# Dummy products first, x split from its banks, an earlier lambda, and a last residual with tokens on partitions

## The chip, the cores and the metric

One core of one Trainium2 chip runs the whole program. The time is device microseconds of one execution; the kernel before takes 1857.08 us (median of 3 runs, 1857.0 to 1858.16).

## The reference

Three pre-norm transformer layers over x (512 tokens, width 1024), all in fp32. What the change touches, cut to that:

```python
# layer 1: forgetting attention beside a multiscale pool, then a gated FFN
h = rmsnorm(x, norm1_g); proj = h @ w_in            # q, k, v, forget logits, pool input u
x = x + concat(attn, pool) @ w_out
x = x + (silu(h2 @ w_gate) * (h2 @ w_up)) @ w_down;  x = rmsnorm(x, final_g)
# layer 2: differential attention; lam needs only four parameter vectors
lam = exp(sum(lq1*lk1)) - exp(sum(lq2*lk2)) + 0.2
a = softmax(s0) - lam * softmax(s1);  o = (a @ v);  x = x + norm(o) @ w_o
# each of layers 2 and 3 ends in a convolutional FFN
x = x + (silu(g) * val) @ w_down                     # w_down: 2816 x 1024
return rms_norm(x, final_norm_g)                     # last step of all
```

## The kernel before

x lies transposed in `XT` (features on partitions, 8 tiles of 128 x 512). Every fp32 product is made of three fp32r products (high x high, high x low, low x high), so each weight chunk and each activation tile is split in a high half (ACT, `whi`/`hi`, lines 1855 and 1859) and a low half (DVE, `wlo`/`lo`, lines 1685, 1676, 1691). Weights come in chunks of up to 128 x 1024 through 2 raw buffers `RAW` and 3 split buffers `WH`/`WL`; SP loads chunk n+2 once `wlo` of chunk n is done. `gemm_f` (lines 1552 to 1554) takes 4 feature blocks of 512 tokens per chunk; `gemm_t` (lines 1580 to 1582) puts tokens on partitions.

All work is written as generators that yield steps. A planner (`run`) gives every step an estimated begin and duration (`takes`, `LAG`) and emits, engine by engine, the one that can begin first, by rank among those that begin within 60 to 100 ns. The result is one fixed order for each engine: an engine executes its steps in that order and waits at the head of its queue if the plan was too hopeful. DMA issues sit in SP's queue in the same emission order.

- Start. PE waits for the identity first of all. `x_in(f)` turns four 128 x 128 blocks of x into a bank (`x_turn`), copies the bank to `XT` (`x_copy_v` or `x_copy_a`), and only then `Norm.feed` makes the halves from `XT` (`make`) and the squares. SP issues x quarter 0, chunk 0 (2 k-blocks), quarter 1, chunk 1, quarters 2 and 3, then some 20 small loads, then chunk 2. Squares are added up on POOL (`acc`, line 1980), `sums` (line 1614) reduces them on PE, `root_in`, `root_exp`, `root_out` make the reciprocal root.
- Pool stretch of layer 1 (about 155 to 185 us). After the last products of the norm, `ev_pool` runs `scaled` (DVE), sliding sums on POOL (`window`, line 1999), `less` and `lo` on DVE for each of four groups; the residual of the first attention group adds 8 banks into `XT` (`add`, line 1697); then `mix` (4 products) and the splits of its banks, on which the next residual waits.
- `lam_sums()` (line 1409 in `products`) is spawned as layer 2 begins: four broadcast loads (line 1533), `lam_in` (two reductions of 128 x 64, line 1813), `lam_exp` (ACT), `lam` (three small DVE operations, lines 1819 to 1822). DVE and ACT wait for its results in line.
- End. The last `ffn` calls `residual`: 144 products into 8 banks, 8 `add`s, 8 squares and POOL sums for the last norm, then `way_out`: `out_turn` (32 transposes of `XT`), 8 `out_scale`s on DVE and 8 stores of 256 KB.

Of the kernel before, what the change touches and what calls it, by code (L numbers as in the profile page):

```python
# [42 lines left out]
    "x_turn": {"pe": 1}, "x_copy_a": {"act": 1}, "x_copy_v": {"dve": 1},  # L43
# [15 lines left out]
    "out_turn": {"pe": 1}, "out_scale": {"dve": 1},  # L59
# [77 lines left out]
def takes(kind, eng, f):  # L137
# [9 lines left out]
    if eng == "pe":  # L147
        if kind == "gemm_f":
            return 3 * len(f["xs"]) * mm(512)
        if kind == "gemm_t":  # L150
            return 3 * len(f["xs"]) * mm(f["width"])
# [11 lines left out]
    if eng == "act":  # L163
# [6 lines left out]
        return {"whi": 1060.0, "tap2": 805.0, "silu": 625.0, "tok_qk": 890.0, "tok_q": 584.0, "tok_k": 482.0, "o_copy": 683.0,  # L170
                "key_row": 710.0, "root_exp": 450.0, "lat_sq": 660.0, "consts": 510.0, "vec": 220.0, "cvec": 470.0, "tok_f": 270.0,
                "gate_exp": 500.0, "lam_exp": 210.0}.get(kind, 600.0)
    if eng == "dve":
        if kind == "lo":
            n = width_of(f["src"])
            return dve(n) if f["scale"] is None else 1.45 * dve(n) if f["src"].shape[0] == P and n == S else 1.1 * dve(n)
# [4 lines left out]
        if kind == "p_two":  # L181
            return 420.0 + 440 + 1.55 * width_of(f["p1"])
        return {"wlo": 1273.0, "add": 682.0, "tap1": 743.0, "tap0": 743.0, "settle": 745.0, "diag": 880.0, "root_in": 165.0,
                "root_out": 760.0, "both_in": 370.0, "both_out": 370.0, "eighth": 170.0, "lam_in": 500.0, "lam": 500.0,
                "gate_in": 400.0, "gate_log": 190.0, "kv_mean": 170.0, "q_root": 170.0, "fg_cols": 160.0}.get(kind, 690.0)
# [5 lines left out]
def build(nc, a, out):  # L191
    with ExitStack() as ctx:
# [183 lines left out]
        def halves(dst_h, dst_l, src, after, scale=None, free=()):  # L376

            hi = yield step("hi", dst=dst_h, src=src, scale=1.0 if scale is None else scale, after=counts([*after, *free]))
            lo = yield step("lo", dst=dst_l, src=src, high=dst_h, scale=scale, after=[hi.act])
            return lo.dve  # L380

        def split_pair(pair, src, after, scale=None, rows=slice(0, P)):
            h, l = pair.h, pair.l
            lo = yield from halves(R[rows, h.i, :], R[rows, l.i, :], src, after, scale, h.free + l.free)
            pair.ready = [lo]
            return lo
# [17 lines left out]
        def plan_qk(w, g, qo, ko):  # L404
            for k in range(0, 8, 2):
                chunk(2, 512, (0, wap(w, k * P, 2, qo + g * 256, 256)), (256, wap(w, k * P, 2, ko + g * 256, 256)))
# [18 lines left out]
        def plan_ffn(part, pieces, down):  # L425
# [3 lines left out]
            plan_rows(down, PARTS[part][0] * 256, 2 * len(PARTS[part]))  # L429

        for g in (0, 1):
            plan_qk(w_in, g, 0, 512)
# [32 lines left out]
        for part in range(len(PARTS)):  # L465
            plan_ffn(part, ((up2[1], 0), (up2[1], 2816)), dn2[1])

        landed, lands, w_split, w_low, w_used = [], {}, {}, {}, {}
        raw_cnt = [0] * NRAW
# [11 lines left out]
        def high_weights(which):  # L481
            for n in which:
                while n >= NSP and n - NSP not in w_used or n >= NRAW and n not in lands:
                    yield None
                free = [w_used[n - NSP]] if n >= NSP else []
                w_split[n] = yield step("whi", n=n, after=[(s_raw[n % NRAW], landed[n]), *free])

        def low_weights(which):
            for n in which:
# [3 lines left out]
                lo = w_low[n] = yield step("wlo", n=n, after=[st.act])  # L493
# [53 lines left out]
        def root(x, n, inv_d, after):  # L547

            v, l, y, c, o = (small(n) for _ in range(5))
            st = yield step("root_in", x=x, v=v, inv_d=inv_d, after=counts(after))  # L550
            st = yield step("root_exp", v=v, l=l, y=y, after=[st.dve])
# [3 lines left out]
        class Norm:  # L555
# [11 lines left out]
            def feed(self, f):  # L567
                if self.split:
# [5 lines left out]
            def make(self, f):  # L574
                yield from fill(self.X[f])
                sc = self.cols[:, f:f + 1] if self.cols is not None else col(self.g + f)
                yield from split_pair(self.X[f], XT[:, f, :], x_done[f], sc)
# [116 lines left out]
        def landing(s, t):  # L694
# [6 lines left out]
                   for s in range(2) for hh in range(4) for x in range(2)]  # L701
# [4 lines left out]
        for q in range(4):  # L706
            landing(s_x[q], (5000.0, 8500.0, 12000.0, 13500.0)[q])
        coming(0, 1700.0)
        coming(1, 5500.0)
# [3 lines left out]

        def x_in(f):
            c = f // 4
            while c and not flags.vec:
                yield None
            b = yield from bank()
            src = [TOK[:, t, f * P:f * P + P] if c == 0 else FS[:, xs2[t].i, (f - 4) * P:(f - 3) * P] for t in range(4)]
            st = yield step("x_turn", bank=b.i, src=src, after=counts([b.free, (s_x[f // 2], 16)]))  # L720
            if f < 4:
                tok_free.append(st.pe)
            if f == 7:
                for x in xs2:
                    fsl.put(x, st.pe)
            if f % 2:
                st = yield step("x_copy_a", f=f, bank=b.i, after=[st.pe])
                x_done[f] = [st.act]
            else:
                st = yield step("x_copy_v", f=f, bank=b.i, after=[st.pe])  # L730
                x_done[f] = [st.dve]
            put_bank(b, *x_done[f])
            while not flags.vec:
                yield None
            N.feed(f)
# [19 lines left out]

        for f in range(8):
            spawn(x_in(f), 0)
        spawn(vectors(0, V_N2), 0)
        spawn(constants(), 1)
        spawn(high_weights(range(1)), 0)  # L760
        spawn(low_weights(range(1)), 0)
        hot += [spawn(high_weights(range(1, len(chunks))), 2), spawn(low_weights(range(1, len(chunks))), 2)]
# [21 lines left out]
        def k_tiles(base):  # L784
            def put(n, bank, done):
# [4 lines left out]
                for (i, r), hi in zip(parts, his):  # L790
                    st = yield step("lo", dst=KT[r, i + 1, :], src=bank[r, :], high=KT[r, i, :], scale=None, after=[hi])
# [368 lines left out]
        def ffn(N, value, nxt):  # L1160
            for part in range(len(PARTS)):
# [5 lines left out]
                if part == len(PARTS) - 1:  # L1167
                    N.free_x(newest_use())
                    N.shut = True
                    yield from residual(Gt, len(Gt), nxt())  # L1170
# [211 lines left out]
        def products():  # L1382
# [7 lines left out]
            N.shut = True  # L1390
            yield from till(A0)
# [17 lines left out]
            spawn(lam_sums())  # L1409
# [37 lines left out]
            def last_norm():  # L1447
                last.n = Norm(split=False, bc=False)
                return last.n
# [620 lines left out]
```

## Time and profile before

| | |
|---|---|
| median of 3 runs | 1857.08 us |
| profiled execution | 1857.17 us, of which the span is 1855.4 us |
| PE busy | 1826.2 us, 98% of the span |
| DVE, ACT, POOL busy | 1135.3, 792.6, 160.7 us |
| PE's first product | 13.12 us; its last 1841.13 us |

Line numbers (L1552) are those of the kernel before. A matmul is issued before the one ahead of it has drained, so its rate is the distance between two starts and not its duration.

### The profile page before, as it was taken

To read this page: it belongs to the slowest core of one execution; us is meant where nothing else is said; L and a number is where in the kernel's file an instruction comes from. 1 tells how busy PE (TensorE), PEld (TensorE's weight loads), DVE (VectorE), ACT (ScalarE), POOL (GpSimd) and SP (SyncE) were. 2 spreads that over 40 slices of the span, in tenths; PEclk is the share of its full clock that TensorE was granted. 3 is DMA by queue.
4 is the path that set the end of the run, shared out by engine and by line. 5 is a ranking of instruction groups with operands and counts; after the bars stand their busy time and mean duration, and the time that the engine had idled before them with its cause. 6 is when DMAs were issued, how large, how long until landed. Compare 5 with 4: busy or idle time off the path is not lost.

```text
span 1855.4 us, 23103 instructions
## 1 busy us (share of the span) xinstructions
PE 1826.2 (98%) x8954; PEld 1517.2 (82%) x8954; DVE 1135.3 (61%) x1886; ACT 792.6 (43%) x1407; POOL 160.7 (9%) x155
## 2 busy tenths in 40 slices
PE   8999999999999999999999999999999999999998
PEld 6897788888888898987888888879888888888886
DVE  4577644344346777768663663665889866366364
ACT  5563332222135555454441432446767544144242
POOL 4003200000004101012000000023010200000002
PEclk9999999999999999999999999999999999999999
DMA  4211223323322221112333333232111133332332
GB/s 147 79 47 55 77 92 101 92 91 95 98 91 94 69 69 57 47 57 86 92 95 91 96 98 91 92 87 69 37 46 35 61 99 95 99 91 92 100 93 80
DMA packets 127961, 152.17 MB, mean 82 GB/s; under 512 B 9258, under 2 KB 100940, under 8 KB 127852
## 3 DMA queue, kind: packets, MB, share of 16 engines
q1 hardware_dynamic: 127692, 150.62, 26.3%
q8 instruction: 71, 1.16, 0.3%
q14 instruction: 38, 0.31, 0.1%
q10 hardware_dynamic: 160, 0.07, 0.0%
HBM read 148.50 MB, written 2.10 MB: 81 GB/s over the span
## 4 chain that ended last, share of the span: by engine, by line
PE 92%; DVE 4%; POOL 2%; issue 1%; ACT 1%; DMA 0%; POOLq 0%; DVEq 0%; ACTq 0%
PE bk L1552 23%; PE bk L1554 23%; PE bk L1553 23%; PE bk L1580 5%; PE bk L1581 5%; PE bk L1582 5%; PE bk L1557 3%; PE bk L1635 1%; PE bk L1637 1%; PE bk L1636 1%; DVE R L1676 1%; PE bk L1614 1%; DVE XT L1697 1%; PE bk L1641 1%; PE bk L1621 1%
## 5 line engine op out<-in xcount | busy, mean ns | idle before, releaser
L1552 PE MATMUL bk<-R,WH 128*128 128x512 f32 x1812 | 720.8, 398 | 9.0 <-DVE WL L1685 4.3
L1553 PE MATMUL bk<-R,WH 128*128 128x512 f32 x1812 | 716.6, 395 | 0.0
L1554 PE MATMUL bk<-R,WL 128*128 128x512 f32 x1812 | 716.5, 395 | 0.0
L1685 DVE TENSOR_TENSOR WL<-RAW,WH 128x1024 fp32r<-128x1024 f32 (+3 forms) x282 | 352.0, 1249 | 542.6 <-ACT WH L1855 541.9
L1855 ACT ACTIVATE WH<-RAW 128x1024 fp32r<-128x1024 f32 (+3 forms) x282 | 293.5, 1042 | 702.2 <-PE bk L1554 640.5
L1552 PEld LDWEIGHTS bk<-R,WH 128*128 128x128 f32 x1812 | 340.4, 188 | 91.5 <-DVE WL L1685 4.7
L1554 PEld LDWEIGHTS bk<-R,WL 128*128 128x128 f32 x1812 | 340.2, 188 | 83.3
L1553 PEld LDWEIGHTS bk<-R,WH 128*128 128x128 f32 x1812 | 340.4, 188 | 80.9
L1980 POOL TENSOR_TENSOR FS<-FS 128x512 f32<-128x512 f32 x56 | 88.7, 1591 | 1252.2 <-ACT FS L1879 1249.9
L1580 PE MATMUL bk<-WH,R 128*128 128x512 f32 (+4 forms) x528 | 188.1, 356 | 2.5 <-DVE R L1676 2.5
L1581 PE MATMUL bk<-WH,R 128*128 128x512 f32 (+4 forms) x528 | 181.2, 343 | 0.0
L1582 PE MATMUL bk<-WL,R 128*128 128x512 f32 (+4 forms) x528 | 181.1, 343 | 0.0
L1697 DVE TENSOR_TENSOR XT<-bk,XT 128x512 f32<-128x512 f32 x160 | 106.2, 684 | 42.6 <-PE bk L1554 42.4
L1676 DVE SCALAR_TENSOR_TENSOR FS<-FS,VEC 128x511 f32<-128x511 f32 (+1 forms) x176 | 121.9, 746 | 8.8 <-ACT FS L1949 8.7
L1580 PEld LDWEIGHTS bk<-WH,R 128*128 128x128 f32 x528 | 100.1, 190 | 12.9 <-issue 3.1
L1582 PEld LDWEIGHTS bk<-WL,R 128*128 128x128 f32 x528 | 100.1, 190 | 11.8
L1581 PEld LDWEIGHTS bk<-WH,R 128*128 128x128 f32 x528 | 100.4, 190 | 9.4
L1921 ACT ACTIVATE FS<-bk,SM 128x128 f32<-128x128 f32 (+3 forms) x160 | 83.5, 527 | 46.4 <-DVE SM L1746 46.0
L1786 DVE TENSOR_TENSOR FS<-bk,FS 128x512 f32<-128x512 f32 x136 | 88.8, 684 | 11.7 <-PE bk L1554 11.7
L1949 ACT ACTIVATE FS<-FS,VEC 128x512 f32<-128x512 f32 x88 | 67.1, 806 | 41.8 <-DVE FS L1786 41.7
L1746 DVE TENSOR_REDUCE SM<-bk 128x1 f32<-128x128 f32 (+3 forms) x160 | 73.2, 482 | 9.1 <-PE bk L1641 8.4
L1859 ACT ACTIVATE PT<-bk 128x128 fp32r<-128x128 f32 (+3 forms) x128 | 53.2, 434 | 36.7 <-PE bk L1557 36.1
(126 smaller groups left out, 1653.6 us busy)
## 6 DMA issues: line engine op xcount, KB each, us to landing
RAW<-in_ffn_w_up_dram SPq DMA_DIRECT2D x176, 256.0 KB, 3.0
RAW<-in_ffn_w_down_dram SPq DMA_DIRECT2D x44, 512.0 KB, 3.8
RAW<-in_w_gate_dram SPq DMA_DIRECT2D x44, 256.0 KB, 2.8
RAW<-in_w_up_dram SPq DMA_DIRECT2D x44, 256.0 KB, 3.1
RAW<-in_w_down_dram SPq DMA_DIRECT2D x22, 512.0 KB, 3.6
RAW<-in_da_w_qkv_dram SPq DMA_DIRECT2D x32, 256.0 KB, 3.0
RAW<-in_w_in_dram SPq DMA_DIRECT2D x17, 256.0 KB, 3.1
RAW<-in_w_out_dram SPq DMA_DIRECT2D x8, 512.0 KB, 3.6
```

Source lines behind the costliest of these rows:

```text
L1552: e.matmul(dst, lh, rh, start=start, stop=False)
L1553: e.matmul(dst, lh, rl, start=False, stop=False)
L1554: return e.matmul(dst, ll, rh, start=False, stop=stop)
L1580: e.matmul(dst, R[:, xh, t], wh[:, j, :], start=st.start and j == 0, stop=False)
L1581: e.matmul(dst, R[:, xl, t], wh[:, j, :], start=False, stop=False)
L1582: mm = e.matmul(dst, R[:, xh, t], wl[:, j, :], start=False, stop=st.stop and j == top)
L1676: return e.scalar_tensor_tensor(out=dst, in0=x, scalar=s, in1=y, op0=o0, op1=o1)
L1685: e.tensor_tensor(WL[:, s, 0:m], RAW[:, r, 0:m], WH[:, s, 0:m].bitcast(F32), ALU.subtract).then_inc(on["wlo_dve"], 1)
L1697: e.tensor_tensor(XT[:, st.m, :], BK[st.bank][:, :], XT[:, st.m, :], ALU.add).then_inc(on["add_dve"], 1)
L1786: e.tensor_tensor(st.dst, BK[st.bank][:, :], st.bc, ALU.mult).then_inc(on["scaled_dve"], 1)
L1855: e.activation(WH[:, s, 0:m], RAW[:, r, 0:m], ACT.Copy).then_inc(on["whi_act"], 1)
L1980: e.tensor_tensor(st.acc, st.acc, st.x, ALU.add).then_inc(on["acc_pool"], 1)
```

## The change

Five things, all in the plan and in a few engine steps:

- `warm()`: products of a zeroed K tile into an unused bank, of lowest rank, as long as the plan has no `gemm_t`. (PE's wait for the identity stays ahead of everything.)
- `x_in`: both halves of x are made from the bank, the copy to `XT` follows; at most 3 banks for turned blocks at first. The first two weight chunks hold 1 k-block each, and both are loaded ahead of x quarter 1.
- `takes`: `whi`/`wlo` are priced by their width; `lo` is dear only where it reads `XT`.
- `lam_sums` is spawned in layer 1, just after the pool's products.
- The last residual is done by `way_out`: w_down's last 6 chunks are all kept (high and low halves in `KT` and `PT`, free by then), products have tokens on partitions, `out_turn` adds `XT` into the same bank by an ordinary fp32 product with the identity, and each block of 128 tokens gets its squares (`out_sq`), root, scale and store by itself, tokens (0, 1), then 2, then 3.

```diff
-        for g in (0, 1):
-            plan_qk(w_in, g, 0, 512)
+            plan_qk(w_in, g, 0, 512, (2, 2, 2, 2) if g else (1, 1, 2, 2, 2))
...
+        def warm():
+            st, i = None, 2
+            b = yield from bank("gemm")
+            ready_at[id(k_zeros[0][0]), k_zeros[0][1]] = 1300.0
+            while not made.get("gemm_t_pe", 0):
+                st = yield step("warm", bank=b.i, i=i, after=[k_zeros[0]])
+            kfree[i].append(st.pe)
+            put_bank(b, st.pe)
...
         def x_in(f):
...
+            yield from fill(N.X[f])
+            cut = yield from split_pair(N.X[f], BK[b.i][:, :], [turned.pe], col(V_N1 + f))
+            spawn(x_copy(f, b, cut))
...
             N.free_x(newest_use())
             N.shut = True
+            spawn(lam_sums())
             yield from till(A0)
...
-            spawn(lam_sums())
...
-            return dve(n) if f["scale"] is None else 1.45 * dve(n) if f["src"].shape[0] == P and n == S else 1.1 * dve(n)
+            return dve(n) if f["scale"] is None else 1.45 * dve(n) if f["from_x"] else 1.1 * dve(n)
...
+            for ts in ((0, 1), (2,), (3,)):
+                bk = {}
+                for t in ts:
+                    for c in (0, 1):
+                        bk[t, c] = yield from bank("gemm")
+                order = range(len(O)) if not ws else [*range(0, len(O), 2), *range(1, len(O), 2)]
+                for j in order:
...
+                    for t in ts:
+                        b = bk[t, c]
+                        st = yield step("gemm_t", n=n, t=t, bank=b.i, width=512, ...)
+                        w_used[n] = b.full = st.pe
+                        if j < 2:
+                            yield step("out_turn", t=t, c=c, bank=b.i, after=counts(x_done[4 * c:4 * c + 4]))
+                for t in ts:
+                    spawn(block_out(t, bk[t, 0], bk[t, 1], gb), 0)
+
+        def block_out(t, b0, b1, gb):
+            for c, b in enumerate((b0, b1)):
+                sq = yield step("out_sq", dst=FS[:, jk.i, 0:S], bank=b.i, z=z[:, c:c + 1], ...)
+                if c == 0:
+                    half = yield step("root_in", x=z[:, 0:1], v=w, inv_d=1.0 / D, after=[sq.act])
+                    gained = yield step("out_gain", dst=TOK[:, t, 0:S], bank=b.i, g=FS[:, gb[0].i, 0:S], ...)
+            st = yield step("out_in", v=v, z=z[:, 1:2], w=w, after=[sq.act, half.dve])
+            r, rooted = yield from root_of(v, 1, st.dve)
+            st = yield step("out_scale", dst=FS[:, o.i, 0:S], bank=b1.i, r=r, g=FS[:, gb[1].i, 0:S], ...)
+            emit("out_store", t=t, c=1, src=FS[:, o.i, 0:S], after=[st.dve])
+            st = yield step("out_root", dst=dst, r=r, after=[gained.dve, rooted])
+            emit("out_store", t=t, c=0, src=dst, after=[st.act])
...
             load(0)
+            load(1)
             e.dma_start(TOK[:, :, 256:512], xq[:, :, 256:512]).then_inc(s_x[1], 16)
-            load(1)
...
                     for f in range(4):
-                        mm = turn(BK[st.bank][:, f * P:f * P + P], XT[:, 4 * st.c + f, st.t * P:st.t * P + P])
+                        mm = e.matmul(BK[st.bank][:, f * P:f * P + P], XT[:, 4 * st.c + f, st.t * P:st.t * P + P], IDN,
+                                      start=False, stop=False)
```

## Rows read from the trace of the kernel before

**Rows 1.** The page: busy time of each engine in us.

```profile
PE 1826.2 (98%) x8954; PEld 1517.2 (82%) x8954; DVE 1135.3 (61%) x1886; ACT 792.6 (43%) x1407; POOL 160.7 (9%) x155
```

**Rows 2.** Waits of PE: line, waited for, us in total, times, longest.

```profile
PE bk L1552 <- DVE WL L1685: 4.3, 1, 4.3
PE bk L1552 <- DVE R L1691: 4.1, 2, 2.5
PE bk L1614 <- POOL FS L1980: 3.8, 3, 2.9
```

**Rows 3.** Timeline of PE, 0 to 20 us: start, us, what, count, idle before.

```profile
13.12 0.77 PE L1580 MATMUL bk<-WH,R 128*128 128x512 f32 x1 [2.51 <-DVE R L1676]
...
14.53 0.63 PE L1580 MATMUL bk<-WH,R 128*128 128x512 f32 x1
14.96 0.63 PE L1581 MATMUL bk<-WH,R 128*128 128x512 f32 x1
...
19.37 0.40 PE L1581 MATMUL bk<-WH,R 128*128 128x512 f32 x1
19.60 0.40 PE L1582 MATMUL bk<-WL,R 128*128 128x512 f32 x1
```

**Rows 4.** DMA issues (KB, us to landing); SP's timeline where chunk 2 begins.

```profile
CN<-in_cst_dram ACTq DMA_DIRECT2D x1, 64.0 KB, 3.4
FS<-in_da_lam_k_dram SPq DMA_DIRECT2D x2, 32.0 KB, 3.4
13.28 11.62 SPq L1489 DMA_DIRECT2D RAW<-in_w_in_dram  x6
```

**Rows 5.** Timeline of DVE, 166 to 183 us.

```profile
173.81 1.54 DVE L1691 TENSOR_TENSOR R<-FS,R 128x512 fp32r<-128x512 f32 x1
...
180.00 2.71 DVE L1676 SCALAR_TENSOR_TENSOR R<-bk,VEC,R 128x512 fp32r<-128x512 f32 x4
```

**Rows 6.** Timeline of POOL, 160 to 178 us.

```profile
170.27 6.23 POOL L1999 TENSOR_TENSOR FS<-FS 128x527 f32<-128x527 f32 x4
```

**Rows 7.** Groups of DVE by line and form: busy us, mean ns, idle before.

```profile
L1685 DVE TENSOR_TENSOR WL<-RAW,WH 128x1024 fp32r<-128x1024 f32 x268 | 339.6, 1268 | 513.5 <-ACT WH L1855 512.9
L1813 DVE CUSTOM_DVE_ANT_0 FS<-FS 128x64 f32<-128x64 f32 x2 | 2.6, 1310 | 0.0
L1819 DVE TENSOR_TENSOR SM<-SM 128x1 f32<-128x1 f32 x1 | 1.2, 1248 | 0.0
L1758 DVE TENSOR_TENSOR SM<-SM 128x1 f32<-128x1 f32 x32 | 5.1, 159 | 1.1
```

**Rows 8.** Windows: stretch, us, busy of PE, PEld, DVE, ACT, POOL, then PEclk.

```profile
226.00:232.00 6.00, 6.00 (x18) 4.72 (x17) 1.62 (x2) 0.00 (x0) 0.47 (x1) 0.61 0.56 175
610.00:617.00 7.00, 7.00 (x30) 5.75 (x29) 3.78 (x17) 2.28 (x5) 0.00 (x0) 0.79 0.36 118
```

**Rows 9.** Timeline of PE at two places: an fp32 product by fours, and the last product.

```profile
235.74 1.05 PE L1621 MATMUL bk<-FS,CN 128*128 128x128 f32 x8
...
1841.13 0.39 PE L1554 MATMUL bk<-R,WL 128*128 128x512 f32 x1
```

**Rows 10.** Timeline of DVE and SP from 1840 us to the end.

```profile
1841.56 0.69 DVE L1697 TENSOR_TENSOR XT<-bk,XT 128x512 f32<-128x512 f32 x1 [0.70 <-PE bk L1554]
1845.71 0.16 DVE L1710 TENSOR_SCALAR SM<-bk 128x4 f32<-128x4 f32 x1 [3.46 <-PE bk L1614]
1847.29 5.36 DVE L1676 SCALAR_TENSOR_TENSOR FS<-bk,SM,FS 128x512 f32<-128x512 f32 x8
1848.07 4.94 SPq L1544 DMA_DIRECT2D out_dram<-FS  x8
```

**Rows 11.** Groups of ACT by form, and the stores' row of DMA issues.

```profile
L1929 ACT ACTIVATE FS<-bk,SM 128x512 f32<-128x512 f32 x8 | 5.5, 683 | 0.0
L1921 ACT ACTIVATION_READ_ACCUMULATOR FS<-bk,SM 128x1 f32 x160 | 32.1, 201 | 0.0
out_dram<-FS SPq DMA_DIRECT2D x8, 256.0 KB, 2.2
```

More of the change, by code:

```diff
@@ L482, in high_weights @@
             for n in which:
-                while n >= NSP and n - NSP not in w_used or n >= NRAW and n not in lands:
+                while NSP <= n < kept and n - NSP not in w_used or n >= NRAW and n not in lands or n >= kept and not Ms[3].valued:
                     yield None
-                free = [w_used[n - NSP]] if n >= NSP else []
-                w_split[n] = yield step("whi", n=n, after=[(s_raw[n % NRAW], landed[n]), *free])
+                free = [] if n < NSP else [w_used[n - NSP]] if n < kept else counts([kfree, ptfree])
+                w_split[n] = yield step("whi", n=n, m=chunks[n][0] * chunks[n][1], after=[(s_raw[n % NRAW], landed[n]), *free])
         def low_weights(which):
@@ L547, in root, with root_of @@
         def root(x, n, inv_d, after):
-            v, l, y, c, o = (small(n) for _ in range(5))
+            v = small(n)
             st = yield step("root_in", x=x, v=v, inv_d=inv_d, after=counts(after))
-            st = yield step("root_exp", v=v, l=l, y=y, after=[st.dve])
+            return (yield from root_of(v, n, st.dve))
+        def root_of(v, n, done):
+            l, y, c, o = (small(n) for _ in range(4))
+            st = yield step("root_exp", v=v, l=l, y=y, after=[done])
             st = yield step("root_out", v=v, l=l, y=y, c=c, o=o, after=[st.act])
@@ L565, in __init__, with feed @@
                 spawn(self.total(), 0)
-            def feed(self, f):
-                if self.split:
+            def feed(self, f, made=False):
+                if self.split and not made:
                     spawn(self.make(f))
@@ L1445, in products @@
             cap["gemm"] = NB
-            def last_norm():
-                last.n = Norm(split=False, bc=False)
-                return last.n
-            yield from ffn(N4, value_conv(1), last_norm)
-            spawn(way_out(last.n), 0)
+            yield from ffn(N4, value_conv(1), None)
         def first_part():
@@ L1588, in tensor_program @@
                     three(BK[st.bank][:, :], wh, wl, R[:, st.x[0], :], R[:, st.x[1], :], True, True).then_inc(on["mix_pe"], 1)
+                elif k == "warm":
+                    for done in st.after:
+                        w.wait_ge(*done)
+                    e.matmul(BK[st.bank][:, :], KT[0:64, st.i, 0:P], KT[0:64, st.i, :], start=True, stop=True).then_inc(on["warm_pe"], 1)
                 elif k == "x_turn":
@@ L1885, in scalar_program @@
                     e.activation(st.y, st.l, ACT.Exp, scale=-0.5).then_inc(on["root_exp_act"], 1)
+                elif k == "out_sq":
+                    for done in st.after:
+                        w.wait_ge(*done)
+                    e.activation(st.dst, BK[st.bank][:, :], ACT.Square, accum_out=st.z).then_inc(on["out_sq_act"], 1)
+                elif k == "out_root":
+                    for done in st.after:
+                        w.wait_ge(*done)
+                    e.activation(st.dst, st.dst, ACT.Copy, scale=st.r).then_inc(on["out_root_act"], 1)
                 elif k == "over_copy":
```

170 lines of the change are left out of this document (108 added, 62 removed).

## The prediction

> **What bounds the kernel now.** I read the page first: PE is busy 98% of the span [rows 1]. So time can come from only two places: from stretches where PE stands still or runs at half clock, and from PE work added or taken away. The waits of PE name the first [rows 2]: 4.3 us once for a weight's low half, 2.5 us once for a low half of an activation, 2.9 us at the end for POOL. The timelines place them. At the start the first product begins at 13.12 us; three such products later two starts lie 0.43 us apart, and 0.23 us apart from 19.37 us on [rows 3]: half and full clock, 1.2 and 2.4 GHz. At about 177 to 182 us DVE works without a gap and PE waits for it [rows 5]. At 225 and 610 us the granted clock falls for a while [rows 8]. At the end 14.3 us lie between the start of the last product (1841.13) and the span's end (1855.4) [rows 9]. The sum is made against the profiled execution, 1857.17 us (span 1855.4 and 1.8 around it); the median of the runs is 0.1 lower.
>
> **Start: -3.2 us.** Before, 6 products are done when full-rate work begins at 19.05 us, after 32 turned blocks (the products of rows 3 and one more each). The change halves what the first product needs: no copy before the halves, and 512 instead of 1024 columns of weights. But two things hold it. PE still waits for the identity, issued at 0.74 us and landed 3.4 us later, 4.1 us [rows 4], while the plan thinks that dummies begin at 1.3 us. About nine dummies (the plan's time up to x, 0.43 us each) stand ahead of the first turned block; at half clock they take 9 x 0.43 = 3.9 us, so the block begins at about 8.4 us and not at 5.8. High half, low half (0.7 us each) and four more dummies bring the first product to about 10.9 us, at full clock by then. The second thing is chunk 2: SP issues it behind all small loads, at 13.28 us [rows 4], and the order of those is untouched. Landed at 17.1 as there (two pieces, 3.9 us from the first issue), split by ACT and then DVE (1.27 us on DVE [rows 7], 1.06 on ACT), it is there at 19.4 us, up to 20.5 if POOL works beside DVE. By then PE has done the 24 products of chunks 0 and 1: 10.9 + 24 x 0.233 + 6 blocks turned x 0.44 = 19.1 us. So at 19.4 to 20.5 us there are 24 products done where there were 6 at 19.05: 18 x 0.233 = 4.2 us, less 0.35 to 1.45. I take 3.2 us. Bounds: 0 (late clock and dummies in the way) and 4.5.
>
> What the clock needs is told by rows only so far: turned blocks and 6 products between 5.8 and 19 us ran at half clock, dense work after them at full. The Trainium skill, "TensorE: Matmul & The Clock Gate", Part 1 and Part 4, says that activity releases a throttle that is the default, and that transposes don't count as it; the trace agrees, and by that rule the dummies open the clock before the first real product. No row shows products of zeros.
>
> **Early lambda, at its old place: -2.0 us.** At 599 us its two reductions of 64 columns take 1310 ns each, and a one-column product 1248 ns where the same form elsewhere takes 159 [rows 7]: POOL is busy beside them, and the squares that end in `sums` stand behind them. PE waits 0.9 us for POOL there (the rest of the 3.8 in rows 2, beside the 2.9 at the end), and then a clock of 0.79 over 7 us [rows 8] is 2.9 us at half rate, 1.5 us lost. Bounds 0.9 and 2.4; I take 2.0, since the gap goes but the thin `sums` stay.
>
> **Early lambda, at its new place: +4.7 us.** It is spawned after the last products of the pool input are emitted, and its rank puts `lam_in` on DVE right behind the second group's `less`, at about 167.5 us, ahead of the residual's adds. POOL works until 176.5 us [rows 6], so the operations cost there what they did at 599: 2 x 1.25 + 1.25 + 0.3 = 4.05 us. DVE has no gap from 167 to 182.7 us, and what comes last on it are the low half at 179.4 (which `mix` waits for) and the four splits from 180.00 [rows 5]. Some of it comes back: two operations that took 1.54 and 1.48 us beside POOL (one in rows 5) now fall behind POOL's end and take 0.7 and 1.2. That leaves a shift of 3.4 us. PE's idle time there grows from 3.5 us to nearly 7, more than the 4.3 us wait at 221 us [rows 2], after which the clock was 0.61 over 6 us [rows 8], 4.7 us at half clock and with the 0.6 us before it 5.3: 2.6 us lost. After the present 2.5 us wait at 177 no clock fell. I count half of it: 3.4 + 1.3 = 4.7. Bounds: 0, if the plan lets adds wait in its stead (DVE is idle 4.6 us after 184, which is what would pay), and 10 (below). Queued behind: ACT waits in line for `lam`, and on it the high halves of the pool.
>
> **The end: -0.3 us.** PE's stream gains the 32 `out_turn` products. Before they are transposes, one record each, and run in the tail while DVE scales. Now they are ordinary fp32 products: the row nearest is `over`, four such products of the same form, 8 records whose starts span 0.78 us, 0.111 us apart [rows 9]. So 32 x 2 x 0.111 = +7.1 us ahead of the last product. The 144 products of the residual stay 144 at 0.233. The tail after the last product's start is rebuilt from rows: 0.43 to the bank's reader (1841.13 to 1841.56 [rows 9, 10]), squares and their sum 0.68 + 0.20 [rows 11], 0.05 gap, root from 1845.71 to 1847.29 = 1.58 and to the first store 0.78 [rows 10], second store 0.40 later, landing 2.2 [rows 11], end 0.5: 6.8 us, against 14.3. So 7.1 - 7.5 = -0.4, and I take -0.3 for the order on ACT. Bounds: -4 (each costs one record, as a transpose does, 3.6 us) and +1 (a wait in the last block). Hidden, at zero: the kept chunks. Their six splits need no free split buffer, 16.8 us of products lie ahead of them, and one passes a raw buffer pair each 3.3 us; without that cover a chunk would cost some 2 us. Eight adds, squares and POOL sums disappear beside PE.
>
> The skill page named above, under Terms, gives transposes of fp32 as 4x faster than the ordinary product. By that rule each `out_turn` would cost 0.44 us, 14 us in all. The trace has 2 x 0.111, so the sum goes by the row.
>
> **Planner's prices.** Cheaper narrow splits and dearer-only-from-`XT` halves reorder queues in places where PE never waits, except at 177 and 221 us; zero, with 1.5 us to either side.
>
> **Sum.** -3.2 - 2.0 + 4.7 - 0.3 = -0.8: 1857.2 - 0.8 = 1856.4, and by the median 1856.3 us.
>
> **Rivals.**
> A, chance 0.42: the forecast, 1856.3, its own range 1853.4 to 1859.5.
> B, 0.28: the plan or the queue absorbs lambda in the pool stretch (0.5 us instead of 4.7). For it: adds wait for nobody on PE at once, and DVE is idle soon after. Against: DVE without a gap for 15 us. Sum -5.0: 1852.1.
> C, 0.12, the other side: lambda's loads. SP issues them behind a weight load, four issues 0.5 us apart, and each lands some 3.4 us later [rows 4]. Issued from 166.4 on, the last lands at about 171.5 us, and DVE, with `lam_in` at the head of its queue since 167.5, stands still 4 us more: 3.4 + 4.0 + 2.6 for the clock = 10.0 in place of 4.7, and the clock at 610 stays (-0.9 instead of -2.0): +5.6, 1862.7. Against it: the load may stand ahead of that weight load. The sum turns to slower than before once lambda's price there passes 5.5 us, and leaves the 0.2% once it passes 9.
> D, 0.11: the first products come no earlier in effect (dummies in front, chunk 2 late, `sums` waiting for POOL as PE is ahead): start 0, sum +2.4, 1859.5.
> E, 0.03: `out_turn` at 0.44 us as by the skill's rule: 32 x 0.22 more, 1863.3.
> F, 0.04: the new order also ends the 4.3 us wait at 221 and the half clock after it (6.9 us): 1849.4 at A's other terms.
>
> A measurement of this kernel tells about 0.2% from no change: 3.7 us, so faster is under 1853.4 and slower over 1860.8. B and F give faster most of their 0.32, A a little: 0.33. C and E, and a tail of D: 0.15. The rest is 0.52. The range that leaves 2 in 10 out is 1850.5 to 1861.5.
>
> **What would show it.** First product near 10.9 us with starts 0.23 apart; chunk 2's split at 19.4 to 20.5 and 24 products before it. Line 1813's successor on DVE near 165 us (all is 3 us earlier) at about 1300 ns each, PE idle 6 to 7 us before the second residual, and a clock under 1 after it. No wait and a clock near 1 at 600 to 617. `out_turn` as 64 records 0.11 apart, 6.8 us from the last product's start to the end. The forecast is wrong if the pool stretch has no more idle PE than before, or the start gains over 4.5 us.

## The result, and the profile after

The changed kernel takes 1860.92 us (median of 19 runs, 1858.91 to 1862.02), the kernel before in the same runs 1857.74 us (19 runs, 1854.98 to 1859.27). The ratio is 1.0019, 95% interval [1.0012, 1.0025]: 3.5 us slower, where 0.8 us less were forecast. The profiled execution took 1861.7 us, its span 1859.9.

The page of the kernel after, first its engines; then PE's waits (line, waited for, us in total, times, longest). They answer to [rows 1] and [rows 2]:

```profile
PE 1836.0 (99%) x8992; PEld 1525.5 (82%) x8992; DVE 1130.3 (61%) x1898; ACT 797.4 (43%) x1426; POOL 151.9 (8%) x148
```

```profile
PE bk L1634 <- DVE R L1779: 5.3, 2, 3.8
PE bk L1634 <- DVE WL L1773: 4.3, 1, 4.3
PE bk L1674 <- DMA CN<-in_cst_dram: 3.7, 1, 3.7
PE bk L1721 <- ACT FS L2024: 0.9, 1, 0.9
PE bk L1639 <- DVE PT L1779: 0.7, 1, 0.7
```

PE is busy 9.8 us more, the wait for `R` grew from 2.5 to 3.8 us at its longest, the one for `WL` stands as it was, and two waits in layer 3 (L1721, L1639) are new. The 2.9 us for POOL at the end are gone.

The start, PE's timeline after, which answers to [rows 3]:

```profile
3.70 3.35 PE L1674 MATMUL bk<-KT 64*128 64x512 f32 x7 [3.70 <-DMA CN<-in_cst_dram]
...
7.18 1.22 PE L1674 MATMUL bk<-KT 64*128 64x512 f32 x2
8.33 1.97 PE L1639 MATMUL bk<-CN,TOK 128*128 128x128 f32 x8
10.23 2.07 PE L1674 MATMUL bk<-KT 64*128 64x512 f32 x4
12.23 1.12 PE L1639 MATMUL bk<-CN,TOK 128*128 128x128 f32 x4
13.00 0.78 PE L1662 MATMUL bk<-WH,R 128*128 128x512 f32 x1
...
17.41 0.44 PE L1663 MATMUL bk<-WH,R 128*128 128x512 f32 x1
17.70 0.40 PE L1664 MATMUL bk<-WL,R 128*128 128x512 f32 x1
```

The products of zeros (L1674) begin at 3.70 us, 0.4 earlier than worked out, and the first turned block at 8.33, as foreseen. But the clock stays at half: the first real product starts at 13.00 us and takes 0.78 us, and only from 17.5 us on do starts lie 0.23 apart. Eight products for turned blocks (L1639) take 1.97 us.

Where time went, by milestones. A kernel's products of weights (7404 in each) are numbered by their start, from 0; the table gives how much later than in the trace of before number n starts, us. So 24 products are done when number 24 starts. All kernels named in it are told below.

| kernel | 24 | 96 | 620 | 850 | 2600 | 5700 | last | end |
|---|---|---|---|---|---|---|---|---|
| before, at us | 23.3 | 42.4 | 174.4 | 240.4 | 652 | 1440 | 1841.1 | 1855.4 |
| after | +1.1 | +0.6 | +0.6 | +3.1 | +2.8 | +5.8 | +12.1 | +4.5 |
| a1_lam_old | +0.7 | +0.2 | +0.2 | +1.2 | +1.2 | +1.4 | +7.7 | +0.1 |
| a2_old_prices | +0.9 | +1.1 | +1.1 | +2.6 | +2.5 | +2.5 | +8.8 | +1.2 |
| a3_no_dummies | -2.5 | -2.3 | -2.3 | +0.8 | +0.5 | +3.0 | +9.3 | +1.8 |
| b1_end_only | -0.6 | -0.6 | -0.6 | +0.6 | +2.1 | +2.1 | +8.4 | +0.8 |
| b2_lam_only | -1.8 | -1.7 | -1.7 | +0.1 | -0.2 | -0.2 | -0.3 | -0.4 |
| c1_live_dummies | -3.4 | -4.0 | -3.9 | -0.8 | -0.9 | +1.6 | +7.9 | +0.3 |
| c2_zero128 | -3.3 | -3.8 | -3.7 | -0.7 | -1.0 | +1.4 | +7.7 | +0.2 |
| c3_live64 | +0.7 | +0.2 | +0.2 | +2.5 | +0.7 | +3.1 | +9.4 | +1.8 |
| c4_mix | -2.9 | -1.5 | -1.5 | -1.6 | -1.6 | -1.6 | +4.8 | -2.8 |
| g3_start_only | +1.3 | +1.5 | +1.5 | +2.9 | +4.6 | +4.6 | +4.6 | +4.5 |
| e3_start128 | -3.6 | -3.4 | -3.4 | -2.7 | -2.7 | -2.9 | -2.9 | -2.9 |
| e1_best | -3.9 | -3.7 | -3.7 | -3.1 | -3.1 | -3.2 | +3.1 | -4.4 |
| e2_best_stock2 | -4.2 | -3.7 | -3.3 | -5.7 | -8.3 | -2.5 | +5.6 | -2.0 |
| g1_prices | -3.5 | -4.1 | -4.0 | -3.3 | -1.6 | +0.9 | +7.2 | -0.4 |
| g2_lam | -4.1 | -3.9 | -3.9 | -3.1 | -4.6 | -4.7 | +1.6 | -5.9 |

So in this one execution: start +0.6, pool stretch +2.5, near 600 us -0.3, layer 3's attention +3.0, end -1.3; together +4.5. One caution goes with every row: after each of the waits near 178, 222 and 607 us the clock is at half for 0, 3.41 or 6.83 us, and which of these it is differs between traces (after had 6.83, 3.41, 3.41; g2_lam 3.41, 3.41, 0). Each 3.41 us costs 1.7. The single column differences behind number 620 are worth no more than that; the times are what decides. The start of before has such a spread too: b1_end_only and b2_lam_only begin as before does, and the clock is full at 18.5 and 15.9 us in them, at 19.0 in before, so that number 96 comes 0.6 and 1.7 us earlier with nothing changed there. The trace of before is the latest of the three, by 0.8 us against their mean, and the column of number 96 flatters every new start by about as much.

The pool stretch, DVE's timeline after (see [rows 5], [rows 7]):

```profile
169.60 1.07 DVE L1901 CUSTOM_DVE_ANT_0 FS<-FS 128x64 f32<-128x64 f32 x1
170.60 0.08 DVE L1901 DVE_READ_ACCUMULATOR2_ANT SM<- 128x1 f32 x1
170.60 0.21 DVE L1901 CUSTOM_DVE_ANT_0 FS<-FS 128x64 f32<-128x64 f32 x1
...
171.35 0.58 DVE L1907 TENSOR_TENSOR SM<-SM 128x1 f32<-128x1 f32 x1
...
181.36 0.68 DVE L1779 TENSOR_TENSOR R<-FS,R 128x512 fp32r<-128x512 f32 x1
```

Lambda's operations take 1.07 + 0.21 + 0.58 + 0.3 = 2.2 us there, not 4.05. PE, which waits for L1779, and the windows after that wait and at 610 us (stretch, us, busy of PE, PEld, DVE, ACT, POOL, PEclk), which answer to [rows 8]:

```profile
182.10 0.80 PE L1634 MATMUL bk<-R,WH 128*128 128x512 f32 x1 [3.77 <-DVE R L1779]
```

```profile
181.00:188.00 7.00, 5.90 (x13) 4.35 (x14) 5.00 (x7) 2.87 (x5) 0.00 (x0) 0.53 0.28 87
610.00:617.00 7.00, 7.00 (x32) 6.00 (x33) 4.02 (x19) 0.83 (x4) 0.00 (x0) 0.76 0.23 75
```

At 600 us lambda's operations are gone from DVE, and the clock still falls. POOL's timeline there, before and after:

```profile
593.25 11.16 POOL L1980 TENSOR_TENSOR FS<-FS 128x512 f32<-128x512 f32 x7 [3.96 <-ACT FS L1879]
605.57 1.28 POOL L1980 TENSOR_TENSOR FS<-FS 128x512 f32<-128x512 f32 x1 [1.17 <-ACT FS L1879]
```

```profile
596.35 13.38 POOL L2083 TENSOR_TENSOR FS<-FS 128x512 f32<-128x512 f32 x8 [3.97 <-ACT FS L1974]
```

Before, POOL waited 1.17 us for the last of its eight sums; after, all eight (13.38 us) stand back to back. The gap that lambda made for the last one was 1.17 us long; PE's own wait for POOL there went from 0.6 to 0.4 us, and its products came 0.3 us earlier.

The end: first one `out_turn` group on PE's timeline, then the timeline of all engines, which answers to [rows 9] and [rows 10]:

```profile
1814.89 1.05 PE L1755 MATMUL bk<-CN,XT 128*128 128x128 f32 x8
1815.70 0.48 PE L1662 MATMUL bk<-KT,R 128*128 128x512 f32 x1
```

```profile
1853.24 0.39 PE L1664 MATMUL bk<-PT,R 128*128 128x512 f32 x1
1853.67 0.60 ACT L1984 ACTIVATE FS<-bk 128x512 f32<-128x512 f32 x1 [4.30 <-PE bk L1664]
...
1855.63 0.16 DVE L1808 TENSOR_TENSOR SM<-SM 128x1 f32<-128x1 f32 x1
...
1856.67 0.33 SPq L1626 DMA_DIRECT2D out_dram<-FS  x1
1857.05 0.43 SPq L1626 DMA_DIRECT2D out_dram<-TOK  x1
```

The tail is 1859.9 - 1853.24 = 6.7 us (14.3 before); the 64 records of `out_turn` lie 0.11 us apart inside a group of 8; the product behind a group starts 0.81 us after the group's first record.

### The profile page after: what moved, and what is told of

It is laid out like the page before. It is cut to its first block, busy times and chain, and to the rows that moved or that the text cites. A ratio compares the mean times of both kernels' runs of the same rounds, so it can differ in the third digit from the quotient of the medians.

```text
span 1859.9 us, 23189 instructions
## 1 busy us (share of the span) xinstructions
PE 1836.0 (99%) x8992; PEld 1525.5 (82%) x8992; DVE 1130.3 (61%) x1898; ACT 797.4 (43%) x1426; POOL 151.9 (8%) x148
## 4 chain that ended last, share of the span: by engine, by line
PE 94%; DVE 2%; ACT 1%; issue 1%; POOL 1%; DMA 0%; DVEq 0%; POOLq 0%; ACTq 0%
PE bk L1634 23%; PE bk L1635 23%; PE bk L1636 22%; PE bk L1662 5%; PE bk L1664 5%; PE bk L1663 5%; PE bk L1639 4%; PE bk L1721 1%; PE bk L1723 1%; PE bk L1722 1%; PE bk L1700 1%; PE bk L1727 1%; PE bk L1707 1%; DVE XT L1785 1%; DVE R L1763 1%
## 5 line engine op out<-in xcount | busy, mean ns | idle before, releaser
L1634 PE MATMUL bk<-R,WH 128*128 128x512 f32 x1764 | 703.0, 398 | 9.6 <-DVE R L1779 5.3
L1635 PE MATMUL bk<-R,WH 128*128 128x512 f32 x1764 | 698.2, 396 | 0.0
L1636 PE MATMUL bk<-R,WL 128*128 128x512 f32 x1764 | 698.2, 396 | 0.0
L1773 DVE TENSOR_TENSOR WL<-RAW,WH 128x1024 fp32r<-128x1024 f32 (+4 forms) x277 | 345.7, 1249 | 539.3 <-ACT WH L1950 538.7
L1950 ACT ACTIVATE WH<-RAW 128x1024 fp32r<-128x1024 f32 (+4 forms) x277 | 287.7, 1039 | 691.7 <-PE bk L1636 630.0
L1634 PEld LDWEIGHTS bk<-R,WH 128*128 128x128 f32 x1764 | 331.8, 188 | 90.6 <-DVE WL L1773 4.7
L1636 PEld LDWEIGHTS bk<-R,WL 128*128 128x128 f32 x1764 | 331.6, 188 | 81.1
L1635 PEld LDWEIGHTS bk<-R,WH 128*128 128x128 f32 x1764 | 332.0, 188 | 78.5
L2083 POOL TENSOR_TENSOR FS<-FS 128x512 f32<-128x512 f32 x49 | 79.9, 1641 | 906.7 <-ACT FS L1974 904.9
L1785 DVE TENSOR_TENSOR XT<-bk,XT 128x512 f32<-128x512 f32 x152 | 100.9, 684 | 28.7 <-PE bk L1636 28.3
L1954 ACT ACTIVATE R<-FS 128x512 fp32r<-128x512 f32 x78 | 48.6, 632 | 48.0 <-DVE FS L1886 22.6
```

The lines of the kernel that those rows point to most:

```text
L1634: e.matmul(dst, lh, rh, start=start, stop=False)
L1635: e.matmul(dst, lh, rl, start=False, stop=False)
L1636: return e.matmul(dst, ll, rh, start=False, stop=stop)
L1773: e.tensor_tensor(low, RAW[:, r, 0:m], high.bitcast(F32), ALU.subtract).then_inc(on["wlo_dve"], 1)
L1785: e.tensor_tensor(XT[:, st.m, :], BK[st.bank][:, :], XT[:, st.m, :], ALU.add).then_inc(on["add_dve"], 1)
L1950: e.activation(home(st.n)[0], RAW[:, r, 0:m], ACT.Copy).then_inc(on["whi_act"], 1)
```

## Experiments: one part at a time

Ratios are against the kernel before, run beside each kernel; x 1857 gives us.

**Without the products of zeros.**

```diff
-        spawn(warm(), 4)
```

> The kernel after without the dummy products. My theory: they don't raise the clock (it rose at 17.5 us after 12 of them), and stand in the way at half clock: 8 ahead of the first turned block (3.1 us) and 4 ahead of the first product (2.0 us). Without them the first turned block begins at 5.2 us, the first product at about 10.5 us instead of 13.0, the clock rises no later than 18 us, and the kernel is 1.5 to 2.5 us faster than after. Rival: they do help the clock; without them full clock comes 3 us later, and the time is equal to or up to 1.5 us above that of the kernel after.

1858.77 us, 1.0009 [1.0, 1.0017]. Its PE timeline:

```profile
5.49 1.97 PE L1638 MATMUL bk<-CN,TOK 128*128 128x128 f32 x8
8.57 1.97 PE L1638 MATMUL bk<-CN,TOK 128*128 128x128 f32 x8 [1.11 <-DMA TOK<-in_x_dram]
10.19 0.78 PE L1661 MATMUL bk<-WH,R 128*128 128x512 f32 x1
...
13.51 0.40 PE L1662 MATMUL bk<-WH,R 128*128 128x512 f32 x1
```

The first product starts 2.8 us earlier than with them, and the clock is full at 13.2 us instead of 17.5. So these products of zeros did not bring the clock; they stood in the way. The ratio is 1.9 us below that of the changed kernel, as expected, though the two intervals overlap (from 1.0012, up to 1.0017).

**Lambda at its old place; the old prices; the end alone.** In the changed kernel:

```diff
             N.shut = True
-            spawn(lam_sums())
...
+            spawn(lam_sums())
```

> The kernel after, with lambda's step spawned at its old place, as layer 2 begins. My theory: the early lambda alone makes the pool stretch longer, by 3.5 us up to product 700, of which 1.0 comes back from a shorter half-clock stretch at 230 us, and gives 0.2 us at 600 us. So this runs 2.3 us below the kernel after (some 1.0 us above before), PE's wait at 178 us is back at 2.5 us and no half clock follows it. Rival: the longer wait at 178 us comes from the cheaper prices or from the turned start; then this is within 0.5 us of the kernel after and the wait stays near 3.8 us.

1857.33 us, 0.9999 [0.999, 1.0007]. PE's wait in the pool stretch is back at 2.5 us as expected, but 3.41 us at half clock follow it all the same.

```diff
-            return ... 1.45 * dve(n) if f["from_x"] else 1.1 * dve(n)
+            return ... 1.45 * dve(n) if f["src"].shape[0] == P and n == S else 1.1 * dve(n)
-        if kind == "wlo": return 175.0 + 1.07 * f["m"]     # whi likewise
+        "wlo": 1273.0                                       # whi: 1060.0
```

> The kernel after, with the planner's old prices (whi, wlo and the low halves as before). My theory: the new prices alone reorder layer 3's attention between 1262 and 1340 us, and that costs the 2.9 us that the trace after loses between products 5280 and 5500, a half clock at 1342 us among it. So this runs 2.9 us below the kernel after. Rival: the order is as good, and the half clock at 1342 us falls by chance in some executions; then this is within 0.7 us of the kernel after, with a half clock there in its trace or a spread of the times as wide.

1858.63 us, 1.0011 [1.0002, 1.002]; 2.9 us less than after were expected. And the kernel before with `way_out`, `block_out` and `out_turn` alone:

> The kernel before with the new end alone: last residual with tokens on partitions, identity products, blocks stored one by one; start, lambda and prices as before. My theory: the products of the identity add 6.4 to 7.1 us ahead of the last product, the tail falls from 14.3 to 6.7 us: 0.5 to 1.3 us faster than before, and nothing else in the trace moves. Rival: the kept chunks' splits, made early, or the later reading of the banks cost a wait elsewhere; then it is equal to before or slower, with PE idle between 1790 and 1840 us.

1856.77 us, 0.9999 [0.999, 1.0008]. By ratios, taking lambda's move back gives 3.7 us (2.3 were expected) and taking the prices back 1.5, which the overlapping intervals (from 1.0012, up to 1.002) don't tell from nothing; the end alone gives nothing that can be measured.

**What the products are made of.** In the changed kernel they are 64 rows of zeros in `KT`. Three variants, each with one or both of these altered:

```diff
-    e.matmul(BK[st.bank][:, :], KT[0:64, st.i, 0:P], KT[0:64, st.i, :], ...)
+    w.wait_ge(s_live, 2)
+    e.matmul(BK[st.bank][:, :], PT[:, 0, 0:P], PT[:, 0, 0:S], ...)     # c3: PT[0:64, ...]
...
+    e.memset(PT[:, 0, 0:S:2].bitcast(F32), 1.40625)                    # c2: 0.0
+    e.memset(PT[:, 0, 1:S:2].bitcast(F32), -2.71875)                   # c2: 0.0
```

Live numbers on 128 rows:

> The kernel after, its dummy products made of live numbers: 128 rows, two values that alternate from column to column, written by two memsets on POOL, in place of 64 rows of zeros. Theory Z: products of zeros don't count as work for the clock, however dense; with live numbers it is full by 8 to 9 us, the last dummies take half the time, the first product begins near 10.7 us at full clock, and the kernel is 2.5 to 3.5 us faster than after. Rival R: dummies don't count because nothing reads them or their bank never changes; then the clock rises at 17 us again and the time is that of the kernel after.

1856.83 us, 0.9997 [0.9989, 1.0006]. Zeros on 128 rows, one execution:

> As the kernel with live dummies, but both memsets write zeros: 128 rows of zeros. Theory Z (the values): the clock rises at 16.5 to 17.5 us as in the kernel after. Rival (it was the 64 rows): the clock is full by 9 us.

1857.32 us. Live numbers on 64 rows, one execution:

> As the kernel with live dummies, but with 64 of the 128 rows. Theory Z (the values alone): full clock by 9 us. Rival (rows count too): the clock rises later than with 128 rows, near 17 us.

1858.99 us. The start of c2_zero128, then of c3_live64, both PE's timeline:

```profile
8.39 1.04 PE L1641 MATMUL bk<-CN,TOK 128*128 128x128 f32 x8
9.18 1.18 PE L1677 MATMUL bk<-PT 128*128 128x512 f32 x4
...
10.64 0.48 PE L1664 MATMUL bk<-WH,R 128*128 128x512 f32 x1
10.96 0.40 PE L1665 MATMUL bk<-WH,R 128*128 128x512 f32 x1
```

```profile
8.17 1.97 PE L1641 MATMUL bk<-CN,TOK 128*128 128x128 f32 x8
10.07 2.07 PE L1677 MATMUL bk<-PT 64*128 64x512 f32 x4
...
12.84 0.78 PE L1664 MATMUL bk<-WH,R 128*128 128x512 f32 x1
13.41 0.63 PE L1665 MATMUL bk<-WH,R 128*128 128x512 f32 x1
```

Zeros on 128 rows: eight turned blocks in 1.04 us, four dummies in 1.18, full clock from 8.3 us. Live numbers on 64 rows: 1.97 and 2.07, full clock from 16.8 us. c3_live64 differs from c1_live_dummies (full clock from 8.25 us) in these rows alone, c2_zero128 in the values alone. So the values play no part; the rows do. That zeros might be the trouble was my theory, and it fell. With its start mended so, the changed kernel (c1_live_dummies) comes to 0.6 us less than before, near the 0.8 that were forecast; that is luck, as its other terms are off by 1.0 to 2.4 us each in its trace, to both sides.

**The best mix without dummies, then with them on 128 rows.** Lambda and prices of before, new start and end; first without `warm`:

> The kernel after without dummies, with lambda at its old place and the old prices: x split from its banks, small first chunks and the new end stay. The parts are independent if my ledger is right: start -2.3 us, end -0.5 to -1.3, nothing else: 3 to 3.5 us faster than before (0.998), the first version that beats it. Rival: the parts meet in the order of layer 1, and the pool stretch or layer 3 takes back over 1 us of it; then it is within 1.5 us of before.

1856.89 us, 0.9995 [0.9986, 1.0004], 0.9 us less where 3 to 3.5 were expected (its profiled execution, 1854.37 us, is one of its faster ones). With zeros on 128 rows:

> The changed kernel with three edits: the products of zeros read 128 rows of a 128-row buffer (in the changed kernel: 64), lambda's sums are back in their old place, and the planner's old prices are back. Theory (rows): the number of rows decides whether the products of zeros open the clock. In the run with zeros on 128 rows the clock was full at 8.33 us, in the changed kernel and in the run with live numbers on 64 rows only at 17.5 and 16.8. So here: full clock from about 8.3 us, 24th product 3.3 us earlier than before, product 5200 about 3.9 us earlier, and no stretch at half clock near 1340, because the prices are the old ones; the end as in the changed kernel (tail 6.7 us, net 1.0 us less); span 1855.4 - 3.9 - 1.0 = 1850.5, against before's time 1853 (ratio 0.9975). Rival (a chip's chance): the early clock in the two runs with 128 rows came from what ran before them and not from the rows; then full clock at about 17, 24th product 0.9 us later, ratio 0.9995 to 1.000 as with no products of zeros at all.

1853.37 us, 0.9981 [0.9972, 0.999], where 0.9975 was expected: 3.5 us under before and 7.1 under the changed kernel. And the start alone, on 128 rows and, as the change has it, on 64:

> The kernel before with the new start alone (products of zeros, halves of x out of its banks, x in quarters), the products of zeros on 128 rows; lambda, prices and the end are those of before. Rows theory: full clock at 8.3 us, 24th product 3.3 us earlier, and that is all that the kernel gains: ratio 0.998 (3.8 us). It also splits the start from the end: the kernel with the new end as well should be another 1.0 us faster if the end's net gain in the traces is real, and the same if it isn't. Rival (chance): 24th product 0.9 us later, ratio 1.0005.

1854.24 us, 0.9987 [0.9978, 0.9995].

> The kernel before with the new start alone, products of zeros on 64 rows as in the changed kernel; lambda, prices and end of before. Against the run with the same start on 128 rows (0.9987). Theory of the rows: clock full only at about 17 us, 24th product 0.7 to 1.1 us later than before, offset from product 96 on about +0.5 us, ratio 1.0000 to 1.0005. Rival: the clock opens at 8 to 9 us here too, 24th product 3.6 us earlier, ratio 0.9987; then the rows weren't what held it.

1861.63 us, 1.0019 [1.001, 1.0028], slower than the 1.0000 to 1.0005 expected. These two differ in a product whose result nobody reads (its rows and, with them, the buffer that it reads: `PT` or `KT`), and by 7.4 us in the medians, 0.0032 in the ratio (5.9 us). The two timelines:

```profile
8.07 1.66 PE L1601 MATMUL bk<-CN,TOK 128*128 128x128 f32 x8
9.49 1.17 PE L1637 MATMUL bk<-PT 128*128 128x512 f32 x4
...
11.39 0.39 PE L1624 MATMUL bk<-WH,R 128*128 128x512 f32 x1
```

```profile
8.61 1.97 PE L1599 MATMUL bk<-CN,TOK 128*128 128x128 f32 x8
10.50 2.07 PE L1634 MATMUL bk<-KT 64*128 64x512 f32 x4
...
13.55 1.22 PE L1634 MATMUL bk<-KT 64*128 64x512 f32 x2
14.70 0.79 PE L1622 MATMUL bk<-WH,R 128*128 128x512 f32 x1
```

At half clock the dummies take twice as long and two more get in (13.55): the first product comes 3.3 us later. By number 96 the distance is 4.9 us. The rival here was that the clock's early opening was chance; in all twelve traces with dummies it goes with the rows (full from 7.8 to 9.4 us in c1, c2, e1, e2, e3, g1, g2; from 16.8 to 17.5 in after, a1, a2, c3, g3).

**Lambda and the prices one at a time.** On the kernel before, lambda's move alone:

> The kernel before with lambda's sums moved to their new place and nothing else. Theory A: the move alone costs what the difference between the changed kernel and the one with lambda at its old place shows, 3.5 us by time: a longer wait of TensorE for VectorE's R at 178 to 182 (3.8 instead of 2.5 us), further half clock there, minus 0.3 us at 600; ratio 1.0010 to 1.0020. Rival B: at before's start the pool stretch is reached with other slack and absorbs the work, as most of it comes back at 221 (wait for the weight's lower half): ratio 1.000, offset at product 850 under 1 us.

1857.4 us, 1.0002 [0.9994, 1.0011]: the 3.5 us that theory A expected are not there. On e1_best, the new prices alone, and lambda's move alone:

> The best kernel so far (products of zeros on 128 rows, lambda and prices of before; 0.9981 of before's time) with the new prices put back, nothing else. Theory: the prices alone cost about 2.5 us: in the traces of all kernels with the new prices the products of layer 3's attention are in another order, TensorE waits for VectorE's PT and ScalarE's FS near 1334 to 1340 us (0.7, 1.0 and 0.4 us) and in five of six a half clock of 6.83 us follows, 3.4 us lost; about +1 us at product 700. Ratio 0.9990 to 0.9995. Rival: those half clocks are chance and the prices cost nothing, 0.9981.

1854.17 us, 0.9984 [0.9976, 0.9993].

> The best kernel with lambda's sums at their new place, prices as before. Theory: with the old prices the move costs what it cost in the kernel before with this move alone, 0.3 to 1.6 us (offset at product 850 +1.8, -0.3 at 600), so lambda's larger cost in the changed kernel (2.5 us and a later half clock) came from it and the prices together. Ratio 0.9984 to 0.9990. Rival: it costs 3.5 us by itself as soon as the start is early, ratio 1.000.

1854.03 us, 0.9978 [0.9968, 0.9987]. Neither costs anything that can be measured by itself: both lie within the interval of e1_best (0.9981), against what was expected of the prices (0.9990 to 0.9995) and of lambda (0.9984 to 0.9990). Both together do: c1_live_dummies, which differs from e1_best by these two (and the numbers in the dummies), has 0.9997, 3.0 us more, give or take 2.3 by the two intervals. That this is more than the sum of the two alone (3.0 against 0.6 and -0.6 us) is not shown by the times, as the four intervals together leave 3.3 us open; the waits show it. PE's waits in three kernels, g1_prices, g2_lam and c1_live_dummies:

```profile
PE bk L1636 <- DVE R L1782: 4.1, 2, 2.5
```

```profile
PE bk L1632 <- DVE R L1778: 4.4, 2, 2.8
```

```profile
PE bk L1636 <- DVE R L1782: 5.3, 2, 3.8
```

The wait in the pool stretch is 2.5 us with the prices, 2.8 with lambda, 3.8 with both, the same as in after. The one-column product of lambda tells of the two orders as well: 0.58 us with the new prices (after, a3, c1), 0.16 or 0.17 with the old (a2, b2, g2). From number 620 to 850 the traces lose -0.1 to 1.4 us with neither (c4, e1, e3, g3, b1), 0.7 and 1.0 with the prices (g1, a1), 0.8 to 1.8 with lambda (g2, a2, b2), 2.3 to 3.1 with both (after, a3, c1, c2, c3). The half clocks of the two waits are in these figures: 10.24 us in all five with both, 10.24 or 6.83 in the others.

**An order that might end the wait at 221 us.** On e1_best:

```diff
-                    s.rank = (0.5 if stock < 1 else 2, s.rank[1])
+                    s.rank = (0.5 if stock < 2 else 2, s.rank[1])
```

> The same kernel, with the planner told that a layer's products of tokens rank as urgent while fewer than two pieces of work (instead of one) are in stock. Theory: this fills the wait of 4.3 us at 221 to 225 us for the lower half of a weight, which is an order question; then the 4.3 us go and with them the 3.4 us that the half clock behind it costs (6.83 us at half): up to 7.7 us less, time near 1846 to 1849. Rival: the order only moves the wait to another place of the same length; time within 1.5 us of the kernel without the edit.

1853.77 us, 0.9983 [0.9974, 0.9992]. PE's timeline:

```profile
848.33 2.04 PE L1706 MATMUL bk<-FS,CN 128*128 128x128 f32 x8 [2.61 <-DVE FS L1828]
...
852.64 0.76 PE L1632 MATMUL bk<-R,WH 128*128 128x512 f32 x1 [2.26 <-DVE R L1778]
```

The 4.3 us wait is gone and number 2600 starts 8.3 us earlier than in before (3.1 in e1_best). Then two longer waits at 848 and 853 us, where e1_best has one of 1.56 us, and 10.2 us of half clock from the first of them on take most of it back: at number 5700 only 2.5 us are left, at the end 2.0 (4.4 in e1_best). The rival holds.

## Why the prediction was wrong, step by step

**Start, -3.2 us: the step that failed.** Its form was right: identity, nine dummies at half clock, then the block. That the block's time fits (8.4 foreseen, 8.33) is in part luck: 4.1 + 3.9 is 8.0, and the dummies began at 3.70 us and, with one small product between them, took 4.6. What failed is "four more dummies bring the first product to about 10.9 us, at full clock by then". With the dummies as written the clock was half until 17.5 us and the first product at 13.00; measured +0.6 us at number 96. The prediction noted that no row showed products of zeros, and put the bound at 0; its doubt was about the values, and the ground was the 64 rows, which the changed kernel's code has in plain sight (`KT[0:64, ...]`). With 128 rows each number of the step holds: first product 10.4 to 11.4 us, number 24 at 19.1 to 20.1 us, 3.3 to 4.2 earlier (against the late trace of before), and by time the start alone is worth 2.4 us (e3_start128, 0.9987). Rival D (the start brings nothing, 1859.5 us) named this outcome with 0.11, dummies in front among its reasons, and it is the one nearest to what came.

The Trainium skill, "TensorE: Matmul & The Clock Gate", Part 1, has the clock follow how busy PE has been. By that rule any dense stream of products would do. In g3_start_only and c3_live64 PE works 9.0 and 9.5 of the 10 us from 3 to 13 us and stays at half clock until 17.4 and 16.8 us, longer than the kernel without dummies (6.6 of these 10 us, full at 13.2); in the seven kernels with 128 rows PE works 9.0 to 9.5 of them as well. So the busy share does not tell the two apart, and the measurement decides.

**Early lambda, new place, +4.7 us.** Right in mechanism and sign, too large (+2.5 in the trace of after), and incomplete. Its own sum has a slip: 4.05 less what comes back (1.54 + 1.48 - 0.7 - 1.2 = 1.1) leaves a shift of 2.9 us and not 3.4. The operations took 2.2 us instead of 4.05, as of the two reductions only the first ran slowly and the product took half of what it took at 599. The wait grew by 1.3 us, not 3.4. The half clock behind it, counted by half, was there in full (6.83 us); but of the eight traces with the wait of before two have 6.83 us there (b1, g3), four 3.41 (a1, e1, e3, g1) and only before and c4 none, so the trace of before had been a lucky execution to read from. Alone it costs nothing measurable (b2, g2); the wait grows by 0.3 us alone and by 1.3 beside the new prices.

**Early lambda, old place, -2.0 us.** -0.3 in the trace of after, and the ground was wrong. PE's wait there was 0.6 us (the rest of the 3.8 in [rows 2] stands at 1243 us) and fell by 0.2: the slow operations on DVE hid behind POOL's eight sums, which are back to back once lambda is gone and set almost the same end. I had taken the slowest engine beside POOL for the late one, where it was POOL itself. But one pair of traces is too few here, as the half clock behind the wait differs. From number 850 to 2600, the eight traces with lambda moved (after, a2, a3, b2, c1, c2, c3, g2) win 0.6 us on average against before, with 3.41 us of half clock in six and none in two; the eight others (without e2) lose 0.6, with 3.41 us in five and 6.83 in three (b1, g1, g3). That makes 1.2 us, inside the bounds of 0.9 and 2.4. Whether the shorter wait brings the shorter half clock, or chance does, stays open.

**Prices, 0 (1.5 to either side).** By time nothing speaks against it (g1_prices, 0.6 us above e1_best, within the noise). "In places where PE never waits" does not hold: in layer 3's attention the new order makes waits of 0.9 and 0.7 us, and in six of seven traces with it (not in a1, which has the same waits) 6.83 us of half clock follow near 1340. From number 2600 to 5700 these six lose 2.4 to 3.0 us, more than the 1.5 allowed, a1 0.3 and the traces with the old prices (without e2) none. By time g1_prices splits in two: seven executions at 1852.2 to 1854.2 us and four at 1856.6 to 1858.2, the profiled one (1856.8) among the four. That fits a half clock that falls in some executions only; no trace of a fast one was kept, so it is not shown.

**The end, -0.3 us.** Right. Each of the eight groups of `out_turn` makes the distance between the products around it 0.89 us longer, 7.1 us in all, as foreseen; the products themselves, with tokens on partitions, start 0.227 to 0.233 us apart instead of 0.233, so that the last one moves by 12.1 - 5.8 = 6.3 us only. Tail 6.7 us, 6.8 foreseen. Net -1.3 in the trace, 0.9999 and 0.9987 against 0.9981 by time: 0 to 1 us.

**The sum.** Forecast -0.8, measured +3.5. In the trace of after the terms miss by +3.8 (start, from -3.2 to +0.6), -2.2 (lambda's new place), +1.7 (its old place), +3.0 (prices) and -1.0 us (end), together 5.3, from -0.8 to +4.5. By time the start's rows are worth 4.1 us (1.0019 against 0.9997) to 5.9, as much as the whole miss of 4.3. The parts don't add up by time: g3_start_only alone has the whole 1.0019, and a1_lam_old, with the same slow start, 0.9999. The two traces, 4.3 us apart (spans 1859.8 and 1855.5), show where. With the old prices two more dummies stand ahead of the first product (14.70 us in g3_start_only, 12.81 in a1_lam_old): 1.3 us at number 96. The half clock near 607 us is 6.83 and 3.41 us long: 1.7. The end of before costs 1.1 us more, the pool stretch in g3_start_only 0.4 more; layer 3 with the old prices gives 0.2 back. How much of the half clock is chance stays open.

## What to carry to other kernels

Give dummy products that are to bring the clock up the 128 rows that real ones have: here 128 did it and 64 did not, and nothing between was tried. Look at the shape of the operand, not only at the engine's busy share, and check by the distance of two starts before the first real product. Work taken off one engine gives time only where nothing else ends at the same place: look at what is back to back beside it. And test two small edits that meet in one stretch together as well as apart; here each alone could not be told from nothing, and both together cost 3.0 us (give or take 2.3). Last, read more than one trace before pricing a half clock: with the same wait in front of it, it lasted 0, 3.41 or 6.83 us.

## What the hardware showed that I had not expected

- Products of 64 rows (0.43 us apart, PE busy 9.3 of the 10 us from 3 to 13 in after) left the clock at half until 16.8 to 17.5 us; without any of them it was full at 13.2 and 13.9 (a3, c4), with the same ones on 128 rows at 7.8 to 9.4. Zeros or live numbers made no difference.
- Lambda's first reduction of 64 columns took 1.07 us and the second, right behind it, 0.21, with POOL's sliding sums running beside both; at 600 us, beside POOL's sums of squares, both took 1.31 [rows 7]. The first is slow and the second fast in six kernels with lambda in the pool stretch (after, a2, a3, b2, c1, g2); why, stays open.
